# The opening of a transformer-layer kernel: modulation weights by column halves, the first two projection chunks by halves of the features

## What is computed

```python
mod = silu(c) @ w_mod + b_mod                       # w_mod: 1024 x 6144, for c and for c_ctx
sh1, sc1, g1, sh2, sc2, g2 = split(mod, 6)
hn = rms_norm(x, norm1_w) * (1 + sc1) + sh1
proj = hn @ w_in                                    # w_in: 1024 x 2832; q, k, v, mLSTM q, k, v, o, gates
y = concat(attention(proj), mlstm(proj)) @ w_out
x = x + g1 * y
hn = rms_norm(x, norm2_w) * (1 + sc2) + sh2
x = x + g2 * (64 experts, 8 per token, and a shared one)(hn)
```

## Time and profile before

| | |
|---|---|
| three runs, us | 641.24, 641.90, 642.45 |
| median, us | 641.9 |
| the profiled execution, us | 643.33 |
| its span (first to last instruction), us | 641.7 |
| TensorE busy | 581.4 us, 91% of the span |
| VectorE, ScalarE, GpSimd busy | 211.7, 167.6, 32.7 us |
| moved by DMA | 252.55 MB, mean 394 GB/s |
| mean granted TensorE clock | 0.974 |

### The profile page before, as it was taken

One profiled execution on the slowest core, in us unless ns is written; L12 is line 12 of the kernel. 1 busy time (PEld: TensorE's weight loads), 2 busy tenths in 40 slices (PEclk: granted clock), 3 DMA queues, 4 the chain that ended last, 5 costly groups with the idle time before them and its releaser, 6 DMA issues.

```text
span 641.7 us, 11143 instructions
## 1 busy us (share of the span) xinstructions
PE 581.4 (91%) x4568; PEld 404.7 (63%) x4568; DVE 211.7 (33%) x479; ACT 167.6 (26%) x308; POOL 32.7 (5%) x78
## 2 busy tenths in 40 slices
PE   0789999999999999989999999596999999998776
PEld 0478777688867576756675757363667676765343
DVE  0287777787832222011212221020121212122104
ACT  3164726672622121111221212010212121212010
POOL 1240210010200000000000000000000000000002
PEclk9989999999999999999999999797999999999779
DMA  8999599989998999999999999999999999999995
GB/s 330 386 332 400 205 367 379 411 314 398 420 388 367 393 422 416 421 422 419 421 421 421 420 421 421 421 421 421 420 421 421 419 422 422 420 420 421 422 386 172
DMA packets 50662, 252.55 MB, mean 394 GB/s; under 512 B 5912, under 2 KB 11680, under 8 KB 26288
## 3 DMA queue, kind: packets, MB, share of 16 engines
q1 hardware_dynamic: 47808, 245.85, 94.5%
q0 software_dynamic: 1840, 4.21, 2.1%
q10 hardware_dynamic: 960, 1.74, 0.7%
HBM read 250.06 MB, written 1.72 MB: 392 GB/s over the span
## 4 chain that ended last, share of the span: by engine, by line
PE 70%; DMA 20%; SPq 4%; ACT 2%; DVE 2%; issue 1%; POOL 0%; POOLq 0%; DVEq 0%; ACTq 0%
PE bank L1286 24%; PE bank L1361 12%; DMA ring<-in_w_up 8%; PE bank L1257 7%; PE bank L1303 7%; DMA ring<-in_w_gate 4%; DMA ring<-in_w_in 4%; SPq L572 3%; PE bank L856 2%; DMA ring<-in_w_mod 2%; PE bank L898 2%; PE bank L906 2%; PE bank L902 2%; DMA ccol<-in_c 2%; PE bank L1019 1%; PE bank L1220 1%
## 5 line engine op out<-in xcount | busy, mean ns | idle before, releaser
L1286 PE MATMUL bank<-ring,xe 128*64 128x256 f32 (+1 forms) x1520 | 176.6, 401 | 10.5 <-DMA ring<-in_w_up 8.7
L1286 PEld LDWEIGHTS bank<-ring,xe 128*64 128x64 f32 (+1 forms) x1520 | 111.0, 132 | 50.4 <-issue 24.8
L1361 PE MATMUL bank<-ring,actT 128*64 128x512 f32 (+1 forms) x384 | 86.6, 627 | 6.8 <-DMA ring<-in_w_down 5.2
L2334 DVE TENSOR_TENSOR act_e<-bank,sil 128x256 f32<-128x256 f32 x26 | 11.0, 424 | 187.9 <-ACT sil L1749 187.9
L2348 DVE SCALAR_TENSOR_TENSOR ylo<-bank,gslot,yhi 128x512 fp32r<-128x512 f32 x50 | 37.5, 751 | 83.9 <-ACT yhi L1762 83.9
L1762 ACT ACTIVATE yhi<-bank,gslot 128x512 fp32r<-128x512 f32 x50 | 34.4, 687 | 116.5 <-PE bank L1361 116.5
L1749 ACT ACTIVATE sil<-bank 128x256 f32<-128x256 f32 x26 | 10.0, 385 | 192.1 <-PE bank L1286 192.1
L1257 PE MATMUL bank<-pone,hhi 128*128 128x256 f32 x200 | 50.0, 288 | 0.0
L1361 PEld LDWEIGHTS bank<-ring,actT 128*64 128x64 f32 (+1 forms) x384 | 25.4, 132 | 37.7 <-issue 37.4
L1257 PE MATMUL bank<-pone,hlo 128*128 128x256 f32 x200 | 48.9, 282 | 0.0
L1286 PE MATMUL bank<-rows_tile,xe 128*64 128x256 f32 (+1 forms) x128 | 34.2, 428 | 9.8 <-DMA ring<-in_w_up 6.3
(11 more groups left out here) (388 smaller groups left out, 838.9 us busy)
## 6 DMA issues: line engine op xcount, KB each, us to landing
ring<-in_w_gate SPq DMA_DIRECT2D x49, 1024.0 KB, 25.0
ring<-in_w_down SPq DMA_DIRECT2D x48, 1024.0 KB, 26.3
ring<-in_w_up SPq DMA_DIRECT2D x46, 1024.0 KB, 26.1
ring<-in_w_mod SPq DMA_DIRECT2D x12, 2048.0 KB, 13.9
ring<-in_w_in SPq DMA_DIRECT2D x5, 2048.0 KB, 16.5
gb<-in_w_up SPq DMA_DIRECT2D x5, 1024.0 KB, 23.8
spare<-in_w_gate SPq DMA_DIRECT2D x4, 1024.0 KB, 26.8
ring<-in_w_out SPq DMA_DIRECT2D x2, 2048.0 KB, 18.8
```

The source lines that it names most:

```text
L1286: ins = mm(bank[6][j * w:(j + 1) * w, part * FE:(part + 1) * FE], xe[:, k, slots], weights[:, k, :], start=(k == 0), stop=(k == KD - 1))
L1361: ins = mm(bank[4 + h][j * w:(j + 1) * w, :], actT[:, f, j * w:(j + 1) * w], weights[:, f, 512 * h:512 * h + 512], start=(f == 0), stop=(f ...
```

## The change

A0 and A1 no longer mean shift and scale. A0 is now the columns 0 to 511 of both, A1 the columns 512 to 1023 of both, so that after A0 the first 512 features of the tokens can be scaled and shifted. Chunks 1 and 0 are projected by halves of the features: the low half (4 blocks) after A0, the high half after A1. The order of loads becomes A0 (two), chunk 1, the low half of chunk 0 (1 MB), A1 (2 MB and two of 1 MB), the high half of chunk 0 (1 MB), chunks 2 and 3 and the rest as before: 20 loads. Slot, semaphore and predecessor of each now stand in three lists; chunk 2 waits for A1's first load, chunk 3 for A1's rows, g1's two loads for chunk 1 and chunk 0. SyncE also waits for chunk 1 to have landed before A1's last load, and for chunk 0's low half before its high half. The loads of c move from SyncE's queue to the head of ScalarE's, those of x ahead of the biases and norms. GpSimd's second group of small loads waits until chunk 2 has landed. bT, and the token transposes of the low half, stand between the two halves of A0's rows. The plan of PSUM banks is rearranged for it.

```diff
-        for what in ("A0", "A1", 1, 0, 2, 3, "g1", 4, "m0", 5, "m1", "g2"):
+        def shift_scale(h, k0, k1):
+            return [(w_mod[:, k0:k1, D * q + 512 * h:D * q + 512 * h + 512], k0 % 4, 512 * q, D) for q in range(2)]
+        SLOT_OF = [2, 3, 0, 1, 2, 3, 3, 1] + 3 * [2, 3, 0, 1]
+        SIGNAL_OF = [2, 3, 0, 1, 2, 3, 0, 1] + 3 * [2, 3, 0, 1]
+        FREED_BY = [None, None, None, None, 0, 1, 1, None, 4, 6, 2, 7] + list(range(8, 16))
+        A1_LAST, C0_HIGH = 6, 7
+        for what in ("A0", 1, 0, "A1", "c0_high", 2, 3, "g1", 4, "m0", 5, "m1", "g2"):
+            if what in ("A0", "A1"):
+                h = MODS.index(what)
+                mod_first[what] = len(loads)
+                loads += [shift_scale(h, 0, 4)] + ([shift_scale(h, 4, 8)] if h == 0 else [shift_scale(h, 4, 6), shift_scale(h, 6, 8)])
...
             def load_chunk(i):
-                if i >= 4:
-                    chunk_free(i - 4)
-                for src, off, w in loads[i]:
+                if FREED_BY[i] is not None:
+                    chunk_free(FREED_BY[i])
+                if i in (A1_LAST, C0_HIGH):
+                    chunk_here(sp, max(j for j in range(i) if SIGNAL_OF[j] == SIGNAL_OF[i]))
+                for src, k, off, w in loads[i]:
...
-                if i == 0:
-                    sp.dma_start(ccol[:, 0, :], t["c_ctx"].rearrange("(p k) -> p k", k=KD)).then_inc(c_loaded, 16)
-                    sp.dma_start(ccol[:, 1, :], t["c"][0].rearrange("(p k) -> p k", k=KD)).then_inc(c_loaded, 16)
...
-            pool.wait_ge(chunk_loaded[last_mod % 4], need[last_mod])
+            chunk_here(pool, A1_LAST)
...
             pool.dma_start(vcache[:, :, :], t["cache_attn_v"][0, 0].rearrange("h t d -> t h d")).then_inc(qk_loaded, 16)
+            chunk_here(pool, proj_chunk[2])
...
+            def project_half(c, h):
...
                 if c == 1:
+                    if h:
+                        pe.wait_ge(w_upper_part, 1)
+                    else:
+                        pe.wait_ge(w_upper, uppers_of(1, 0))
                     for s in range(NST):
-                        for b in (s, s + 2):
-                            pe.wait_ge(x_upper[b], 1)
+                        pe.wait_ge(x_upper[s + 2 * h], 1)
                         upper_upper(s)
-                    pe.wait_ge(first_rest, 1)
+                    pe.wait_ge(w_rest, rests_of(1, h))
                     for s in range(NST):
-                        for k in range(KD):
-                            mm(ps[s][:, 0:w], xhi[:, k, s * P:s * P + P], proj_rest(c)[:, k, :], start=False, stop=False)
+                        upper_rest(s, False)
                     for s in range(NST):
-                        pe.wait_ge(x_rest, s + 1)
...
+                        pe.wait_ge(x_rest, NST * h + s + 1)
+                        ins = rest_upper(s, True)
...
+            def turn_opening():
+                pe.wait_ge(consts, 2)
+                pe.wait_ge(col_loaded, 48)
+                ps = claim("bT")
+                complete("bT", nc.tensor.transpose(ps[:, 0:8 * KD], bnr[:, :], ident[0:8 * KD, 0:8 * KD]))
+                transpose_tokens(0)
+
             pe.wait_ge(c_silu, 1)
-            transpose_tokens(0)
-            mod_rows("A0")
+            mod_rows("A0", turn_opening)
             complete("cA0", mod_columns("A0", "cA0"))
+            project_half(1, 0)
+            project_half(0, 0)
+            transpose_tokens(1)
             mod_rows("A1")
             complete("cA1", mod_columns("A1", "cA1"))
-            transpose_tokens(1)
-
-            project(1)
-            project(0)
+            project_half(1, 1)
+            project_half(0, 1)
             project(2)
...
-            token_upper(0)
-            act.wait_ge(chunk_loaded[proj_chunk[1] % 4], need[proj_chunk[1]])
-            A(proj_upper(1)[:, 0:4, :], proj_weights(1)[:, 0:4, :], ACT.Copy).then_inc(w_upper, 1)
+            act.wait_ge(ab_ready, 1)
             token_upper(1)
-            for b in (0, 1, 3):
-                token_exact(b)
+            chunk_here(act, proj_chunk[1])
+            A(proj_upper(1)[:, 0:HK, :], proj_weights(1)[:, 0:HK, :], ACT.Copy).then_inc(w_upper, 1)
+            token_exact(1)
+            chunk_here(act, proj_chunk[0])
+            A(proj_upper(0)[:, 0:HK, :], proj_weights(0)[:, 0:HK, :], ACT.Copy).then_inc(w_upper, 1)
+            rows_out("A1")
+            act.wait_ge(ab_ready, 2)
+            token_upper(3)
+            token_exact(3)
+            chunk_here(act, C0_HIGH)
+            A(proj_upper(0)[:, HK:KD, :], proj_weights(0)[:, HK:KD, :], ACT.Copy).then_inc(w_upper, 1)
...
+            mod_half(0)
...
+            token_upper(0)
+            chunk_here(dve, proj_chunk[1])
+            V.tensor_copy(proj_upper(1)[:, HK:KD, :], proj_weights(1)[:, HK:KD, :]).then_inc(w_upper_part, 1)
...
+            rest_of_weights(dve, 1, 0)
+            token_full(0)
             token_rest(0)
             token_rest(1)
-            dve.wait_ge(chunk_loaded[proj_chunk[0] % 4], need[proj_chunk[0]])
-            V.tensor_copy(proj_upper(0)[:, 6:8, :], proj_weights(0)[:, 6:8, :]).then_inc(w_upper_part, 1)
+            rest_of_weights(dve, 0, 0)
+            rest_of_weights(dve, 1, 1)
+            V.memset(rows[:, :, :], 0.0)
+            chain(V.memset(gi[:, :, :], 0.0))
+            mod_half(1)
+            token_upper(2)
+            token_full(2)
+            token_rest(2)
+            token_rest(3)
+            rest_of_weights(dve, 0, 1)
```

More of the change, by code:

```diff
@@ L401, in mod_loads @@
         def mod_loads(q):
-            return [[(w_mod[:, 4 * a:4 * a + 4, D * q:D * q + D], 0, D)] for a in range(2)]
+            return [[(w_mod[:, 4 * a:4 * a + 4, D * q:D * q + D], 0, 0, D)] for a in range(2)]
+        def shift_scale(h, k0, k1):
[4 more added lines that the diff above has]
+        A1_LAST, C0_HIGH = 6, 7
         mod_first = {}
@@ L859, in mod_rows @@
                         ins.then_inc(chunk_used, 1)
+                        if between is not None:
+                            between()
                 complete(f"r{name}", ins)
@@ L869, in mod_columns, with transpose_tokens @@
                 return ins
[L871 to L874 removed]
+            def transpose_tokens(h):
+                for s in range(NST):
+                    pe.wait_ge(xn_ready, s + 1)
+                    b = s + 2 * h
                     ps = claim(f"xT{b}")
@@ L892, in project @@
                 w = CHUNKS[c][1]
-                pe.wait_ge(w_upper, ORDER.index(c) + 1)
+                pe.wait_ge(w_upper, uppers_of(c))
                 ps = [claim(f"pj{c}_{s}") for s in range(NST)]
+                for s in range(NST):
+                    tok = slice(s * P, s * P + P)
+                    for k in range(KD):
+                        mm(ps[s][:, 0:w], xhi[:, k, tok], proj_upper(c)[:, k, :], start=(k == 0), stop=False)
+                    for k in range(KD):
+                        mm(ps[s][:, 0:w], xlo[:, k, tok], proj_upper(c)[:, k, :], start=False, stop=False)
+                    pe.wait_ge(w_rest, rests_of(c))
+                    for k in range(KD):
+                        ins = mm(ps[s][:, 0:w], xhi[:, k, tok], proj_rest(c)[:, k, :], start=False, stop=(k == KD - 1))
+                    complete(f"pj{c}_{s}", ins)
@@ L904, in upper_rest, with rest_upper @@
-                def upper_rest(s):
-                    for k in range(KD):
+                def rest_upper(s, last):
+                    for k in ks:
+                        ins = mm(ps[s][:, 0:w], xlo[:, k, s * P:s * P + P], proj_upper(c)[:, k, :], start=False,
+                                 stop=(last and k == KD - 1))
+                    return ins
+                def upper_rest(s, last):
+                    for k in ks:
                         ins = mm(ps[s][:, 0:w], xhi[:, k, s * P:s * P + P], proj_rest(c)[:, k, :], start=False,
-                                 stop=(k == KD - 1))
-                    complete(f"pj{c}_{s}", ins)
+                                 stop=(last and k == KD - 1))
+                    return ins
@@ L942, in qk_transposes @@
+                for s in range(NST):
+                    ins = upper_rest(s, True)
+                    if h:
+                        complete(f"pj{c}_{s}", ins)
             def qk_transposes(s):
@@ L1865, in gate_rows_out, with mod_half @@
                 drain(f"r{name}", V.tensor_tensor(rsb[:, MODS.index(name), :], ps[0:MR, 0:MW], brow[:, name == "g2", :], ALU.add))
+            def mod_half(h):
+                ps = product(dve, f"cA{h}")
+                v = slice(HK * h, HK * h + HK)
+                for q in range(2):
+                    out = modc[:, q, v, :].rearrange("p (c j) s -> p c j s", j=MW // P)
+                    src = ps[:, 0:MW].rearrange("p (j c r) -> p c j r", j=MW // P, c=CT)[:, 2 * q:2 * q + 2, :, 0:NST]
+                    bias = bcol[:, q, v].rearrange("p (c j) -> p c j", j=MW // P)
```

(6 more changed lines are left out.)

144 lines of the change are left out of this document (66 added, 78 removed), and 2 rows, old and new, of the table plan.

## The result

| | before | after |
|---|---|---|
| runs | 6 | 6 |
| median, us | 641.86 | 648.60 |
| lowest to highest, us | 641.24 to 642.45 | 646.08 to 650.02 |
| profiled execution, its span, us | 643.33, 641.7 | 649.75, 648.1 |
| mean granted TensorE clock | 0.974 | 0.965 |

Ratio 1.0099, 95% interval 1.0083 to 1.0114: 6.7 us slower, where 0.7 was forecast and the range ended at 645.0.

The account below looks back on a forecast made before the run. Weights streaming at the pace of slot release bound the long expert part, so the opening's shift carries to the end: scores +1.4, less 0.7 absorbed, gives +0.7 us on 641.9, or 642.6 us; range 640.0 to 645.0.

Parts of the forecast that it names:

- the opening's gain: Projection halves: 8 us of earlier start shrink to 1.3 us at chunk 0's end, which nothing later uses.
- the scores 1.4 us later: Attention scores: start 1.4 us later than before, because they wait behind chunk 4's landing and rounding.
- a queue lag of 4.3: DMA queue in the opening: pause of 5.3 us less 1 given back, net 4.3 us, bounds 2.5 and 6.5.
- The forecast's 74.3: Chunk 4's transfer: issued at 63.6, it flows until 73.5 and lands at 74.3 instead of 72.90.
- the small loads fill the pause: Queue pause from 35 to 40.3: GpSimd's first small loads fall there and give back 0.3 to 2 us, taken as 1.
- 2 KB pieces: Loads of w_mod: reading rows in 2 KB instead of 4 KB pieces costs zero, on rates of 409 against 407 GB/s.
- The lower clock in the halves: Pauses at 22 to 25.6 and 41 to 43.5: rival's loss of 1.7 us, mostly swallowed by chunk 1's VectorE wait.
- 52.5 for chunk 0's end: End of the late halves: chunk 0's projection done at 52.5 us, against 53.77 before.
- some 3 us: Before the attention scores: TensorE idles some 3 us.
- Given back: Stream behind the scores: TensorE arrives 1.4 us later and finds m1 landed, so 0.7 us is absorbed.
- the statements of what would prove it wrong: Opening: chunk 4 landing by 72, A1's rows before 37, or the clock dropping in chunk 0's halves.
- The rival with the lower clock: Opening: clock loss of 1.7 us delays chunk 4, scores +3.1, end 644.3; chance 0.22, shared with the lag's upper bound.

Follow-up runs that it names:

- 1: The changed kernel with ScalarE making the two copies before rounding chunk 4: 644.21 us, ratio 1.0030.
- 2: The changed kernel with the 1 MB expert tile issued behind chunk 4 instead of ahead of it: 644.65 us, ratio 1.0032.
- 6: The changed kernel with 8, 14 and 10 unused identity transposes in TensorE's pauses around the tokens: 649.15 us, ratio 1.0105.
- experiment 4: The changed kernel with 24 unused identity transposes on TensorE in the pause before the scores: 647.29 us, ratio 1.0076.
- 8: The kernel before, with SyncE issuing chunk 2 only when chunk 1's second product is done: 644.54 us, ratio 1.0025.
- 7: The changed kernel without GpSimd's wait for chunk 2 before its second group of small loads: 647.67 us, ratio 1.0090.
- 5: The changed kernel with the first 32 of A1's row matmuls ahead of chunk 0's low half: 647.73 us, ratio 1.0088.
- 9: The kernel before, with A0's and A1's loads each read as two transfers in 2 KB pieces: 644.50 us, ratio 1.0026.
- 3: The changed kernel with both the copies before chunk 4's rounding and the expert tile behind chunk 4: 643.74 us, ratio 1.0028.
- 10: The changed kernel with A1's first rows early, transposes in the token pauses, copies first and tile behind chunk 4: 641.97 us; without the transposes 645.06.
- 11: The kernel before, with GpSimd's small loads later: 642.07 us; with 20 transposes ahead of project(1): 643.56; with both: 643.71.

## Why the prediction was wrong

The path was the one forecast: the opening's gain had no taker, the queue fell behind, chunk 4 came late, and the late chunk reached the scores by way of ScalarE's order. That is shown by experiments 1, 2 and 6. The sizes failed, all to one side. The sum had the scores 1.4 us later by a queue lag of 4.3, and nothing for what follows the idle time before them. Measured were 5.1 by a lag of 6.5, and 1.6 more behind the idle time.

- **The lag of the queue: 4.3 counted, 6.5 measured.** The lag shows at the expert tile ahead of chunk 4, which landed at 72.6, not at 66.1 + 4.3 = 70.4:

```profile
56.24 0.56 SPq L616 DMA_DIRECT2D spare<-in_w_gate  x1
```

```profile
spare<-in_w_gate SPq DMA_DIRECT2D x1, 1024.0 KB, 16.4
```

  Chunk 4 landed 5.4 behind the tile. The forecast's 74.3 leaves only 3.9 between the two, although it counts 5.15 for 2 MB elsewhere. These are the 3.7 us between 74.3 and 78.0. The transit came out as counted (10.7 and 11.06) by luck: issue and landing were late by nearly the same.
- **What did not set it.** Chunk 4's own issue came at 66.96 instead of 63.6, but with the 7.95 us of the empty queue it would by estimate have landed at 74.9; the bytes ahead of it decided. Nor did the lower clock in the halves decide: the execution of experiment 4 issued chunk 2 at 38.83, where the forecast had it, ended chunk 0 at 53.9 and got chunk 4 only 0.6 earlier, and experiment 6 ended chunk 0 at 52.8 and got it 0.5 earlier.
- **What made up the 6.5** is known in part. The pause alone, in the kernel before, moved the tile by 2.6 (8); GpSimd's second loads behind chunk 2 have a part of up to 1.8 (7); so has the late release of chunk 2's slot: with chunk 2 issued at 34.1 (5), the tile landed at 70.8, 1.8 earlier. These parts overlap, and the rest stays open. The prediction let the small loads fill the pause and give back 1; what the trace has there is a share of 0.38 at 49 GB/s.
- **2 KB pieces, put at zero.** 386 GB/s over 4 to 16 us against 409 in the same window of the kernel before; alone 1.7 us (9). The inference rested on a misread row: the window 52 to 56 with its 409 GB/s held little of w_in. Chunk 3, the last of it, landed at 53.46, and what flowed for the rest was g1, rows of w_mod in 4 KB pieces. In the kernel before, chunks of w_in flow from 48 on and the 4 KB pieces alone from 56 to 60:

```profile
48.00:52.00 4.00, 4.00 (x19) 3.24 (x19) 0.71 (x3) 3.63 (x1) 0.00 (x0) 1.00 1.05 392
...
56.00:60.00 4.00, 4.00 (x19) 3.27 (x18) 3.14 (x7) 1.93 (x1) 0.00 (x0) 1.00 1.03 410
```

  Over 48 to 50, w_in alone, it is 387. The Trainium skill (Perfetto Trace Analysis, DMA Optimizations) says that batching 2 KB transfers into 4 or 8 KB can raise throughput much. The prediction set it aside on that row; the runs agree with its direction, at 6%. A0's first rows started at 12.38 instead of 11.0, chunk 1's low half at 26.60 instead of 25.6.
- **The lower clock in the halves, put into a rival at 1.7 us and partly swallowed.** A0's second rows took 3.50 us for 32 matmuls where 1.93 was counted. Chunk 1's low half ended at 32.4, not 30.0, 1.4 of which came after its late start; its high half at 50.2, not 46.6. The argument that VectorE's pace would hide it was wrong. So "52.5 for chunk 0's end" was 55.8; rows and tokens between the halves cost no more than was counted (3.63 us of 3.9, 1.4 to scaled tokens of 1.6). In the change this lateness lay hidden under chunk 4's; it shows where chunk 4 is off the path (3, 10).
- **The scores started 5.1 later, not 1.4**, and chunk 4's landing is all of it: 78.0 against 72.9. The 2.0 of chunk 0 don't add to it; before the scores TensorE still idled 3.76 us.
- **The lower clock behind the idle time before the scores** stood nowhere in the sum: the prediction saw "some 3 us" of idle time there and did not ask what follows it. Scores and g1's rows took 1.6 us more; the trace of experiment 4 has these 1.6 back.
- **Given back.** 0.7 was counted. The wait before m1's second rows is gone, and the first expert begins 5.5 us later than before (185.35 against 179.85), so 1.2 of the 6.7 were absorbed; the span is 6.4 longer all the same. Where the 0.9 between went, in the expert part, wasn't tried and stays open.

Of the statements of what would prove it wrong, none came true to the letter: chunk 4 landed late, A1's rows came at 40.8, and over chunk 0's halves the clock was at its higher level but for the first instants of the low one. It had dropped in chunk 1's halves, just ahead. The rival with the lower clock had the nearer number, 644.3, and saw one of the places where the clock falls; but it had this make chunk 4 late, and experiments 4 and 6 speak against that: with the clock up there, chunk 4 landed only 0.5 to 0.6 earlier.

## What to carry to other kernels

When a change splits work to start it earlier, list the idle times that the splitting makes on TensorE, and price what follows each at the lower clock, also those far behind the edit. Follow a late load back through what was queued ahead of it before blaming its own issue. In a ring whose slots are released by one engine, mending one release can move the gap to the next; test edits to such a chain in combination, since one alone may show nothing (6), and take each out of the combination again, since one in it may be worth nothing. Before a window's rate is taken for a kind of transfer, look which transfers it holds. An instruction for data that may be late doesn't belong ahead of ready copies on which another engine waits.

## What the runs showed of the hardware

Of TensorE's pauses before the scores, those of 0.63, 0.78, 0.97, 1.04, 1.30, 1.43 and, once, 1.80 us left the clock at 2.4 GHz (16 score matmuls in 1.7 us); those of 1.91, 2.95, 3.03, 3.76 and 3.89 were followed by the 1.2 GHz level, for part or all of the scores (2.1, 2.3, 2.1, 2.4 and 3.1 us). The Trainium skill (TensorE: Matmul & The Clock Gate, HAM oscillation) says that idling between bursts brings the clock down; the runs agree. Transposes whose results nobody reads held it up (10 against the same kernel without them), for the most part (6), or turned the saving into a longer pause elsewhere (11). The same code, with the same pause of 1.62 us before the token transposes, had its next 32 row matmuls in 3.50 us in one execution and in 1.93 in another (the change and experiment 4); what decides between the two isn't known here.

Over 12 to 24 us w_mod flowed at 410 GB/s in 4 KB pieces (the kernel before) and at 386 in 2 KB pieces (9). Chunks of w_in, in 2 KB pieces, flowed at 387 (48 to 50 us) and 401 (68 to 70) in the kernel before. A load of 2 MB into an otherwise empty queue took 7.95 to 9.25 us from issue to landing (chunk 4 in the kernel before and its variants with the small loads later, the transposes, or both).

The least expected result is in 11: chunk 0's end 0.8 us earlier, and a kernel 1.3 us slower.
